# Gate and up projections of a two-layer encoder as seven block products in place of eight

## What is computed

```python
def _swiglu(x, wg, wu, wd):
    return (jax.nn.silu(x @ wg) * (x @ wu)) @ wd
...
    for l in range(DEPTH):
        h = x + 0.5 * _swiglu(_rmsnorm(x, ffn1_norm[l]), ffn1_wg[l], ffn1_wu[l], ffn1_wd[l])
        u = _rmsnorm(h, mix_norm[l])
        p = u @ w_in[l]
        ...
        h = h + jnp.concatenate([ret, dif], axis=-1) @ w_out[l]
        h = h + 0.5 * _swiglu(_rmsnorm(h, ffn2_norm[l]), ffn2_wg[l], ffn2_wu[l], ffn2_wd[l])
        x = _rmsnorm(h, final_norm[l])
```

## Time and profile before

| | us |
|---|---|
| three runs | 1997.11, 1997.98, 1999.52; median 1997.98 |
| the profiled execution | 1998.23 |
| its span, first to last instruction | 1996.4 |
| PE busy, PEld busy | 1955.0, 1608.2 |
| POOL, DVE, ACT busy | 856.0, 732.5, 700.0 |
| granted TensorE clock, share of full | 0.993 |

### The profile page before, as it was taken

How to read it: one execution, slowest core, us unless ns; L and a number is a source line. 1 busy time by engine, 2 the same in 40 slices (tenths; PEclk the granted TensorE clock), 3 DMA queues, 4 the chain that set the end, 5 groups by cost and what they waited for, 6 DMA issues and landing times.

```text
span 1996.4 us, 24454 instructions
## 1 busy us (share of the span) xinstructions
PE 1955.0 (98%) x8698; PEld 1608.2 (81%) x8698; DVE 732.5 (37%) x1007; ACT 700.0 (35%) x997; POOL 856.0 (43%) x388
## 2 busy tenths in 40 slices
PE   9999999998899999999999999999989999999997
PEld 7888888886688888888878888888767888888886
DVE  4212332428575221212442124233485642122125
ACT  5322333445434322322532223234454243222224
POOL 4444443453334444444344444435433344444442
PEclk9999999999999999999999999999999999999999
DMA  4323232321122232222233222323211133222222
GB/s 149 130 98 114 96 110 90 100 97 62 49 68 86 97 103 96 95 95 93 91 103 117 95 95 95 105 82 109 85 53 53 53 106 105 96 95 95 95 95 74
DMA packets 54965, 186.00 MB, mean 93 GB/s; under 512 B 6440, under 2 KB 7976, under 8 KB 54860
## 3 DMA queue, kind: packets, MB, share of 16 engines
q1 hardware_dynamic: 53136, 181.61, 27.5%
q10 hardware_dynamic: 1724, 2.96, 0.5%
HBM read 182.44 MB, written 3.15 MB: 93 GB/s over the span
## 4 chain that ended last, share of the span: by engine, by line
PE 91%; DVE 5%; issue 3%; ACT 1%; DMA 0%; SPq 0%; DVEq 0%; ACTq 0%; POOL 0%; POOLq 0%
PE bank L457 20%; PE bank L459 20%; PE bank L458 20%; PE pair L457 7%; PE pair L459 7%; PE pair L458 7%; DVE neg_max L1184 1%; PE bank L479 1%; PE bank L475 1%; PE bank L476 1%; PE pair L672 1%; PE bank L687 1%; ACT s L933 1%; PE pair L506 1%; PE pair L501 1%
## 5 line engine op out<-in xcount | busy, mean ns | idle before, releaser
L415 POOL TENSOR_TENSOR w_lo<-raw,w_hi 128x1024 fp32r<-128x1024 f32 (+1 forms) x344 | 810.1, 2356 | 1088.4 <-ACT w_hi L745 1088.2
L745 ACT ACTIVATE w_hi<-raw 128x1024 fp32r<-128x1024 f32 (+1 forms) x344 | 355.5, 1034 | 680.3 <-PE bank L459 511.7
L457 PE MATMUL bank<-hg_hi,w_hi 128*128 128x512 f32 x1128 | 445.6, 395 | 0.0
L458 PE MATMUL bank<-hg_lo,w_hi 128*128 128x512 f32 x1128 | 440.6, 391 | 0.0
L459 PE MATMUL bank<-hg_hi,w_lo 128*128 128x512 f32 x1128 | 440.4, 390 | 0.0
L457 PE MATMUL bank<-a_hi,w_hi 128*128 128x512 f32 x768 | 299.5, 390 | 0.0
L458 PE MATMUL bank<-a_lo,w_hi 128*128 128x512 f32 x768 | 298.8, 389 | 0.0
L459 PE MATMUL bank<-a_hi,w_lo 128*128 128x512 f32 x768 | 298.8, 389 | 0.0
L457 PE MATMUL pair<-hg_hi,w_hi 128*128 128x512 f32 x656 | 255.2, 389 | 0.0
L458 PE MATMUL pair<-hg_lo,w_hi 128*128 128x512 f32 x656 | 255.2, 389 | 0.0
L459 PE MATMUL pair<-hg_hi,w_lo 128*128 128x512 f32 x656 | 255.2, 389 | 0.0
(11 more groups left out here) (181 smaller groups left out, 1480.7 us busy)
## 6 DMA issues: line engine op xcount, KB each, us to landing
raw<-in_w_gu SPq DMA_DIRECT2D x176, 512.0 KB, 3.3
raw<-in_w_dn SPq DMA_DIRECT2D x64, 512.0 KB, 3.2
raw<-in_w_p SPq DMA_DIRECT2D x56, 512.0 KB, 3.2
raw<-in_w_dn SPq DMA_DIRECT2D x32, 384.0 KB, 3.0
raw<-in_w_o SPq DMA_DIRECT2D x16, 512.0 KB, 3.2
out_y<-h SPq DMA_DIRECT2D x8, 256.0 KB, 2.1
h<-in_x ACTq DMA_DIRECT2D x4, 256.0 KB, 5.5
h<-in_x SPq DMA_DIRECT2D x4, 256.0 KB, 6.4
```

Source lines behind the costliest of these rows:

```text
L415: pool.tensor_tensor(w_lo[:, s, 0:tiles, :].rearrange("p a b -> p (a b)"), raw[:, s % RAW, 0:n], w_hi[:, s, 0:tiles, :].rearrange("p a b - ...
L457: pe.matmul(out, w_hi[:, s, k, :], m_hi, start=first, stop=False)
L458: pe.matmul(out, w_hi[:, s, k, :], m_lo, start=False, stop=False)
L745: act.activation(w_hi[:, s, 0:tiles, :].rearrange("p a b -> p (a b)"), raw[:, s % RAW, 0:tiles * P], ACT.Copy).then_inc(hi_done, 1)
```

## The change

The first two tiles of each FFN (`CLASSIC`) stay as they were. The other 20 take gate and up together as a product of 2x2 blocks. The activations fall into A11, A12 (batch one, feature tiles 0 to 3 and 4 to 7) and A21, A22 (batch two); the weights into B11, B21 (gate, feature tiles 0 to 3 and 4 to 7) and B12, B22 (up). With S1 = A21 + A22, S2 = S1 - A11, S3 = A11 - A21, S4 = A12 - S2, T1 = B12 - B11, T2 = B22 - T1, T3 = B22 - B12 and T4 = B21 - T2, seven products P1 = A11 B11, P2 = A12 B21, P3 = S4 B22, P4 = A22 T4, P5 = S1 T1, P6 = S2 T2, P7 = S3 T3 give gate and up of both batches by sums. A product is four feature tiles by three matmuls of 256 columns: 84 matmuls of 256 columns for a tile, in the order P1, P6, P2, P5, P7, P4, P3.

The S are made once for each FFN from `h`, by ACT and DVE beside the first two tiles (`mix_terms`, `mix_sums`, `mix_high`, `mix_low`); S4 takes the place of A21 in `hg_hi`, `hg_lo`, after the last classic product. The T are made for each tile: T1 and T3 by POOL in the raw buffer (`differences`), T2 and T4 by DVE in a bank of PSUM (`t_sum`), which ACT has filled with T1 (`copy_t1`). T2 and T4 share half a slot: ACT writes T4's high part when P6 has ended (`hi_t4`). Each is split into high and low. DVE makes the sums of the products, and multiplies by the norm's factor once for the gate and once after the multiplication of gate and up.

Two more raw buffers (`raw_x`) and two more slots (`w_hi_x`, `w_lo_x`) lie over memory that only the attention uses. The loops over tiles and layers are written out. The down projection puts the last hidden tile of output tiles 0 and 1 behind the others of both. The scaling of `h` by the final norm of layer 0 moves into the adding of the next layer's first chunk. The norm's matmul stands between the first two products (after the third only at the kernel's start), and banks are renamed.

```diff
--- before.py
+++ after.py
+CLASSIC = 2
+FAST = NF - CLASSIC
+KH = KD // 2
+DOWN_SLOT = (0, 1, 2, 3, 4, 5, 3, 4)
+SLOT_AFTER_DOWN = {0: 0, 1: 1, 2: 2, 3: 6, 4: 7, 5: 5}
+FAST_SLOTS = ((0, 1, 2), (3, 4, 5))
...
-        gated = [banks[6], banks[7]]
+        gated, t_sum = banks[6], banks[7]
...
+        prod = {1: banks[0][:, 0:SEQ], 2: banks[1][:, 0:SEQ], 6: banks[1][:, SEQ:T], 5: banks[4][:, 0:SEQ],
+                7: banks[4][:, SEQ:T], 3: banks[5][:, 0:SEQ], 4: banks[5][:, SEQ:T]}
...
+        def raw_block(c, i, which, half):
+            source = raw_x if place(c, i) % 2 == 0 else raw
+            at_ = (2 * which + half) * KH * P
+            return source[:, at_:at_ + KH * P]
...
+            def lo_gate(l, f, c, i):
+                m = fast_index(f, c, i)
+                pool.wait_ge(g_hi, at(g_hi, l, m + 1))
+                hi, lo_ = w_tiles(FAST_SLOTS[place(c, i) % 2][0])
+                pool.tensor_tensor(columns(lo_), raw_tiles(RAW_AT["t", m, 0], UT), columns(hi).bitcast(F32),
+                                   ALU.subtract).then_inc(g_lo, 1)
+            def differences(l, f, c, i):
+                m = fast_index(f, c, i)
+                key = ("t", m, 1)
+                pool.wait_ge(raw_in[RAW_AT[key]], at(raw_in[RAW_AT[key]], l, 16 * (RAW_NTH[key] + 1)))
+                pool.wait_ge(g_lo, at(g_lo, l, m + 1))
+                b11, b12, b22 = raw_block(c, i, 0, 0), raw_block(c, i, 1, 0), raw_block(c, i, 1, 1)
+                pool.tensor_tensor(b11, b12, b11, ALU.subtract).then_inc(t1_done, 1)
+                pool.wait_ge(t1_done, at(t1_done, l, m + 1))
+                pool.tensor_tensor(b12, b22, b12, ALU.subtract).then_inc(t13_done, 1)
+            def lo_differences(l, f, c, i):
+                m = fast_index(f, c, i)
+                pool.wait_ge(t13_hi, at(t13_hi, l, m + 1))
+                hi, lo_ = w_tiles(FAST_SLOTS[place(c, i) % 2][1])
+                both = (raw_x if place(c, i) % 2 == 0 else raw)[:, :].rearrange("p (a b) -> p a b", a=2)[:, :, 0:KH * P]
+                pool.tensor_tensor(columns(lo_).rearrange("p (a b) -> p a b", a=2), both,
+                                   columns(hi).rearrange("p (a b) -> p a b", a=2).bitcast(F32),
+                                   ALU.subtract).then_inc(t13_lo, 1)
+            def lo_b22(l, f, c, i):
+                m = fast_index(f, c, i)
+                pool.wait_ge(b22_hi, at(b22_hi, l, m + 1))
+                hi, lo_ = w_tiles(FAST_SLOTS[place(c, i) % 2][2], KH, KH)
+                pool.tensor_tensor(columns(lo_), raw_block(c, i, 1, 1), columns(hi).bitcast(F32),
+                                   ALU.subtract).then_inc(b22_lo, 1)
...
+                for c, n in enumerate(CHUNKS):
+                    chunk_opening(l, f, c)
+                    for i in tiles_in(c):
+                        if i + 1 < n:
+                            lo_differences(l, f, c, i + 1)
+                            lo_b22(l, f, c, i + 1)
+                        if i + 2 < n:
+                            lo_gate(l, f, c, i + 2)
+                            differences(l, f, c, i + 2)
+                        elif i + 2 == n:
+                            lo(l, down_unit(f, c, 0))
+                    for k in range(1, KD):
+                        lo(l, down_unit(f, c, k))
...
+            def fast_product(q, w, half, m_hi, m_lo):
+                for k in range(KH):
+                    last = three(prod[q], (w, KH * half + k), m_hi[:, k, :], m_lo[:, k, :], k == 0, k == KH - 1)
+                last.then_inc(p_done[q], 1)
+            def blocks_of(rows, half):
+                tokens = slice(rows * SEQ, (rows + 1) * SEQ)
+                ks = slice(half * KH, (half + 1) * KH)
+                return hg_hi[:, ks, tokens], hg_lo[:, ks, tokens]
...
+            def p1(l, f, c, i):
+                m = fast_index(f, c, i)
+                pe.wait_ge(g_lo, at(g_lo, l, m + 1))
+                if c + place(c, i):
+                    pe.wait_ge(p1_copied, at(p1_copied, l, m))
+                else:
+                    pe.wait_ge(gate_ready, at(gate_ready, l, tile_of(f, 0, 0) + 1))
+                fast_product(1, FAST_SLOTS[place(c, i) % 2][0], 0, *blocks_of(0, 0))
+            def p6(l, f, c, i):
+                m = fast_index(f, c, i)
+                pe.wait_ge(x_lo, at(x_lo, l, 2 * m + 1))
+                pe.wait_ge(mix_lo_done, at(mix_lo_done, l, 8 * f + 6))
+                if c + place(c, i):
+                    pe.wait_ge(u2_done, at(u2_done, l, m))
+                else:
+                    pe.wait_ge(up_ready, at(up_ready, l, CLASSIC * f + 1))
+                fast_product(6, FAST_SLOTS[place(c, i) % 2][2], 0, *mixture(2))
+            def p2(l, f, c, i):
+                fast_product(2, FAST_SLOTS[place(c, i) % 2][0], 1, *blocks_of(0, 1))
+            def p5(l, f, c, i):
+                m = fast_index(f, c, i)
+                pe.wait_ge(t13_lo, at(t13_lo, l, m + 1))
+                pe.wait_ge(mix_lo_done, at(mix_lo_done, l, 8 * f + 8))
+                if c + place(c, i):
+                    pe.wait_ge(c22_done, at(c22_done, l, m))
+                fast_product(5, FAST_SLOTS[place(c, i) % 2][1], 0, *mixture(1))
+            def p7(l, f, c, i):
+                fast_product(7, FAST_SLOTS[place(c, i) % 2][1], 1, *mixture(0))
+            def p4(l, f, c, i):
+                m = fast_index(f, c, i)
+                pe.wait_ge(x_lo, at(x_lo, l, 2 * m + 2))
+                if c + place(c, i):
+                    pe.wait_ge(c12_done, at(c12_done, l, m))
+                fast_product(4, FAST_SLOTS[place(c, i) % 2][2], 0, *blocks_of(1, 1))
+            def p3(l, f, c, i):
+                m = fast_index(f, c, i)
+                pe.wait_ge(b22_lo, at(b22_lo, l, m + 1))
+                fast_product(3, FAST_SLOTS[place(c, i) % 2][2], 1, *mixture(3))
+            def down_part(l, f, c, k, ks):
+                n = CHUNKS[c]
+                if ks[0] == 0:
+                    pe.wait_ge(lo_done, at(lo_done, l, down_unit(f, c, k) + 1))
+                    if k >= 2:
+                        pe.wait_ge(h_ready, at(h_ready, l, down_output(f, c, k - 2) + 1))
+                pe.wait_ge(a_ready, at(a_ready, l, tile_of(f, c, ks[-1]) + 1))
+                for i in ks:
...
+            def ffn(l, f):
+                classic_tiles(l, f)
+                for c, n in enumerate(CHUNKS):
+                    for i in tiles_in(c):
+                        p1(l, f, c, i)
+                        p6(l, f, c, i)
+                        p2(l, f, c, i)
+                        p5(l, f, c, i)
+                        p7(l, f, c, i)
+                        p4(l, f, c, i)
+                        p3(l, f, c, i)
+                    down_part(l, f, c, 0, range(0, n - 1))
+                    down_part(l, f, c, 1, range(0, n - 1))
+                    down_part(l, f, c, 0, range(n - 1, n))
+                    down_part(l, f, c, 1, range(n - 1, n))
+                    for k in range(2, KD):
+                        down_part(l, f, c, k, range(0, n))
...
+            def fast_tile(l, f, c, i):
+                n = CHUNKS[c]
+                if place(c, i):
+                    silu(l, f, c, i - 1)
+                copy_p1(l, f, c, i)
+                hi_t4(l, f, c, i)
+                if place(c, i):
+                    hi_gated(l, f, c, i - 1)
+                if i + 1 < n:
+                    copy_t1(l, f, c, i + 1)
+                    hi_differences(l, f, c, i + 1)
+                    hi_t2(l, f, c, i + 1)
+                    hi_b22(l, f, c, i + 1)
+                    if i + 2 < n:
+                        hi_gate(l, f, c, i + 2)
+                    else:
...
+            def mix_terms(l, f, r):
+                if r:
+                    act.wait_ge(mix_lo_done, at(mix_lo_done, l, 8 * f + 2))
+                elif f:
+                    act.wait_ge(h_ready, at(h_ready, l, len(CHUNKS) * KD + KD))
                 else:
+                    act.wait_ge(acc_next_done, at(acc_next_done, l, KD))
+                for k in range(KH):
+                    act.activation(mix_sum[k // 2][:, (k % 2) * SEQ:(k % 2 + 1) * SEQ], h[:, KH * r + k, SEQ:T], ACT.Copy,
+                                   scale=hg_gain(l, f, KH * r + k)).then_inc(mix_term, 1)
+            def mix_high(l, f, r):
+                for half in range(2):
+                    act.wait_ge(mix_sum_done, at(mix_sum_done, l, 4 * KH * f + KH * r + 2 * half + 2))
+                    if r == 3:
+                        act.wait_ge(gu_done, at(gu_done, l, 2 * CLASSIC * (f + 1)))
+                    act.activation(mixture(r)[0][:, 2 * half:2 * half + 2, :],
+                                   mix_sum[half].rearrange("p (a b) -> p a b", a=2), ACT.Copy).then_inc(mix_hi_done, 1)
...
+            def mix_sums(l, f, r):
+                for k in range(KH):
+                    if r < 2:
+                        dve.wait_ge(mix_term, at(mix_term, l, 2 * KH * f + KH * r + 2 * (k // 2) + 2))
```

(35 more changed lines are left out.)

832 lines of the change are left out of this document (548 added, 284 removed).

## The result

| | us |
|---|---|
| before, beside the change | 1997.11, 1997.98, 1999.52 |
| the change, four runs | 1960.44 to 1963.26, median 1962.26 |
| ratio of the change to before, 95% interval | 0.9817, 0.9801 to 0.9832 |
| forecast | 1918, range 1904 to 1972 |
| the profiled execution of the change, its span | 1963.26, 1960.6 |

A fourth execution of the kernel before took 4716.65 us and stands in no figure here.

A forecast was written before the change was run, and what follows sets the result against it. The prediction took PE, busy 98% of the span, as the bound. A saving of 101 us less 2, 10, 4 and 5 left 80, so 1998 - 80 = 1918 us, range 1904 to 1972.

The forecast's parts named there:

- Term 1: Fast tiles on PE: 256-column matmuls 0.1145 us apart, a tile 9.62 instead of 10.88, 80 tiles save 101 us.
- rival B: Pace of 256-column matmuls: the excess is fixed, 0.1201 us each, tiles 10.09, kernel 1945 us; chance 22%.
- The eight short matmuls: Eight 128-column matmuls, each with its own weight load, read as 0.111 us apiece: lower bound for the 256-column pace.
- The half-clock rows: 512-column matmuls at 1.2 GHz, 0.43 us apart without excess, read as leaning to a column-rate limit, 0.1133 for 256 columns.
- Term 2: Other engines in fast tiles: POOL-ACT-POOL loop 10.3 us, longer than PE's 9.62; costs 2 us in chunks of 8, 10 in openings.
- Term 3, down: Down projection: output 2 waits for bank 0 to be emptied, 0.35 us in each of 12 chunks, 4 us.
- All other matmuls stay: Assumption that matmuls outside the 80 changed tiles keep their cost.
- Term 3, openings: Very first opening: P6 starts at 43.6 instead of 39.1, costing 5 us; the other three openings cost nothing.
- a sign of being wrong: The forecast would be wrong if PE waits at other places (P5, P1), or the pace differs through instruction issue.
- C: Helper engines set the pace in all tiles, loop 10.3 to 10.6 us, kernel 1961 to 1985; chance 17%.
- D: Weight loads do not overlap short streams on PE: 0.19 us a pair, a tile 16.0, kernel 2400; chance 10%.
- E: The saving isn't there: pace of 256-column matmuls 0.1275 to 0.131 us, kernel within 0.2%; chance 3%.

The follow-up runs named there:

- the cut outputs: Changed kernel with the 512 columns of single down outputs cut into pieces (256+256, 4x128, 384+128, 448+64), each its own matmul and weight load: 2010.88 us.
- the padding: Changed kernel with 96 bytes of padding, so extra weight slots and block sums begin at a multiple of 128 bytes: 1960.11 us, ratio to before 0.9805.

## Why the prediction went wrong, step by step

| term | forecast | found |
|---|---|---|
| 1, pace: 80 tiles | +101 (tile 9.62) | +70 (tile 10.00) |
| 2, chunks of 8 and last chunks | -2 | 0 |
| 2, first chunks | -10 | -3.4, second FFNs |
| 3, down projection | -4 | -11 (0.99 x 8 + 0.83 x 4): 5 for the bank, 6 for the place of weights |
| 3, openings of the first FFNs | -5 | -18 (10.8 in layer 0, 7.2 in layer 1) |
| sum | 80 | 38 |

From PE's first matmul on `hg_hi` (in layer 1's first FFN from the end of the FFN before it) to the end of the last down phase, the four FFNs take 365.7, 360.0, 362.7 and 360.0 us before and 362.1, 346.7, 355.0 and 347.3 after, 37 in all; the other stages take 1.3 more, and the spans differ by 35.8.

**Term 1 failed where I chose between two bounds.** "I take 0.1145, nearest to the rows with a load each 0.111 us, with a little for the fixed part": measured were 0.119 in the change and 0.120 with all operands on a multiple of 128 bytes. The excess is fixed, as rival B had it (0.1201), and the cut outputs showed 0.111 to be a separate floor. The eight short matmuls are of type fp32, at two cycles a column, and say nothing of fp32r's excess. The trace of before could have shown that, in the attention:

```profile
558.84 1.89 PE L687 MATMUL bank<-s,v 128*128 128x256 f32 x8
```

The last of these is 0.38 long, so they start (1.89 - 0.38) / 7 = 0.216 apart: 0.003 above two cycles a column, 0.2133, where fp32r has 0.0134 above a stream of the same length. The half-clock rows were read as leaning to a limit in columns per time; they fit a fixed time that the slower stream covers, which the same paragraph had named. At half clock 256 columns are 0.213 apart (48.38 to 48.60), without excess too, so such rows could never tell the two apart. This is 31 of the 44 us. The Trainium skill (TensorE: Matmul & The Clock Gate, Back-to-back issue gap) has 262 cycles for 256 columns, 0.109 us; the averages here are 0.116 to 0.122, so the trace doesn't agree for this type either.

**Term 2 was right in its mechanism** (loop 10.48, forecast 10.3; lead in chunks of 8; first chunks short of it) and over-priced, because it was set against a tile of 9.62. At 10.00 the lag is 0.5 a tile. The waits of 0.3 to 0.4 at P6 in the second FFNs (689, 700, 710, and from 1645 on) are it; in the first FFNs the stall at P6 itself gave the helpers their lead, and where the norm's operands in PSUM took layer 1's stall away, these waits came there too (tiles of 10.5).

**Term 3, down:** the wait is the forecast's (0.31 against 0.35). Missing was the place of the weights: outputs 4, 5 and 7 at 0.231 to 0.238. "All other matmuls stay" was an assumption that the padding refuted.

**Term 3, openings:** "P6 starts at 43.6": 48.0. The DVE row taken for the norm's multiplications, 0.70, came from a stretch in which POOL was idle. In the change POOL works just there, which adds 2.8 us, and all behind waits with it. Of the other 1.6, 0.5 is a later opening (the third product's last matmul starts at 30.50, before at 29.98). The rest is DVE's own list: a block sum's low parts (L1437, to 32.90) stand ahead of the norm's first step, which began at 31.27 before. With one operand in PSUM the factor still ended at 36.21 and P6 started at 44.99. The late factor also held the first gate product, whose bank P1 needs: a wait of 2.3 at P1, one of the places that the forecast had named as a sign of being wrong. "In the other three openings ... no cost, thin cover": the cover held in the second FFNs; in layer 1's first FFN the same two rows and a late start of S1's terms (ACT rounds a gate unit that lands at 988.4 first) used it up, 4.55 us from start to start. And no line had a price for what follows a wait, 2.0 and 2.4 us at half clock.

Of the rivals, B gave 1945 with the smaller terms as forecast; with pace, loop and edges as found it is 1945 - 7 + 2 + 7 + 13 = 1960, 2 us below the measured 1962. That the time lies in the stated range is in part luck: the range was opened upward for B and C, while the 20 us (7 + 13) of the down projection and the openings were in no case's sum. C, that the helpers set the pace in all tiles, is refuted by tiles of 10.00 without waits; D, E by the pace. The change itself does what it says.

## What to carry to other kernels

Before cutting matmuls to save arithmetic, take the pace at the new size from a run or bound it by the fixed excess, not by a row whose operation differs in size and type: here seven eighths of the columns cost 0.919 of the time, not 0.875. A helper's row holds only beside the neighbours it had: look at what other engine works in that stretch after the change, and which operand may lie in PSUM. When an operation is moved into an idle slot, follow what its end releases, the transfer above all.

## What the runs showed of the hardware that I had not expected

- A matmul of type fp32r with 128 weight columns costs the larger of columns / 2400 + 0.0133 us and 0.111 us, in the sums of all five ways of taking 512 columns. At half clock the excess is absent (0.213 for 256 columns).
- Weights that begin 32 bytes behind a multiple of 128 bytes make 512 columns cost 0.231 to 0.238 instead of 0.227; streamed activations there 0.234. At 256 columns block sums at that place come at 0.116 to 0.120, 0.118 on average, instead of 0.120, when the weights lie on the multiple; when both lie 32 bytes behind, as in the change's other slots, at 0.120. The cause is open.
- DVE's multiplication with both operands in SBUF took 2.61 and 1.58 us beside POOL, and 0.69 and 0.68 with one in PSUM.
- Behind 4.3 us of idle time PE ran at 1.2 GHz for 25 matmuls; with the time filled by matmuls it stayed at 2.4 GHz. Behind 2.3 us of idle time it ran at 2.4 GHz in the change and at 1.2 GHz in another run.
